# Five vector instructions at the opening of a feed-forward given to GpSimd

## What is computed

```python
    x = x + rmsnorm(ox @ p['x_wo'], nrm[3])
    h = rmsnorm(x, nrm[4])
    u, fconv_new = causal_dwconv(h @ p['f_wu'], fconv, p['f_conv_w'], p['f_conv_b'])
    x = x + rmsnorm((jax.nn.gelu(u) * (h @ p['f_wg'])) @ p['f_wd'], nrm[5])
```

## Time and profile before

| | us |
|---|---|
| median of three runs | 2245.98 (2242.68 to 2252.88) |
| the profiled execution, its own time | 2251.43 |
| its span, first to last instruction | 2249.4 |
| TensorE busy | 2160.9 (96%) |
| VectorE busy | 1285.9 (57%) |
| ScalarE busy | 841.4 (37%) |
| GpSimd busy | 619.2 (28%) |

### The profile page before, as it was taken

One profiled execution on the slowest core, in us unless ns is written; L12 is line 12 of the kernel. 1 busy time (PEld: TensorE's weight loads), 2 busy tenths in 40 slices (PEclk: granted clock), 3 DMA queues, 4 the chain that ended last, 5 costly groups with the idle time before them and its releaser, 6 DMA issues. The chain is left out here.

```text
span 2249.4 us, 42839 instructions
## 1 busy us (share of the span) xinstructions
PE 2160.9 (96%) x17101; PEld 1972.5 (88%) x17101; DVE 1285.9 (57%) x2350; ACT 841.4 (37%) x1720; POOL 619.2 (28%) x519
## 2 busy tenths in 40 slices
PE   9999998989999989999999999998899999999997
PEld 6799977866656689999999988998899999999997
DVE  5213354357776741232255254577898978866957
ACT  5222253126656730111343133554433334334453
POOL 5000035422323022111112200332344443345643
PEclk9999999879999999999999999998999999999998
DMA  4321097983545131110401354332232332264234
GB/s 145 107 61 44 29 204 243 311 284 124 167 135 171 71 120 43 61 57 29 162 29 38 121 198 188 99 114 86 91 124 91 105 110 72 106 238 170 93 125 146
DMA packets 133714, 276.35 MB, mean 123 GB/s; under 512 B 24626, under 2 KB 79571, under 8 KB 128332
## 3 DMA queue, kind: packets, MB, share of 16 engines
q1 hardware_dynamic: 110796, 232.32, 31.0%
q0 software_dynamic: 10368, 28.33, 3.9%
q10 hardware_dynamic: 12352, 12.96, 1.8%
HBM read 229.49 MB, written 48.26 MB: 123 GB/s over the span
## 5 line engine op out<-in xcount | busy, mean ns | idle before, releaser
L88 PE MATMUL psum<-merged_high,oq_half 128*128 128x352 f32 x768 | 189.0, 326 | 1.8 <-POOL oq_half L69 1.4
L88 PE MATMUL psum<-ff_t,ff_x_slots 128*128 128x264 f32 x1200 | 149.1, 284 | 1.3 <-DVE ff_x_slots L69 1.3
L88 PEld LDWEIGHTS psum<-ff_t,ff_x_slots 128*128 128x128 f32 x1200 | 147.1, 188 | 1.6 <-issue 1.5
L88 PEld LDWEIGHTS psum<-merged_high,oq_half 128*128 128x128 f32 x768 | 135.2, 190 | 2.5 <-POOL oq_half L69 1.9
L2006 ACT ACTIVATE na_pt<-psum 128x512 f32<-128x512 f32 (+1 forms) x170 | 86.8, 545 | 106.3 <-PE psum L1881 89.9
L88 PE MATMUL psum<-x_half_high,mg_w_high 128*128 128x352 f32 x384 | 124.0, 323 | 2.0 <-ACT gated L2390 1.2
L88 PE MATMUL psum<-h_again_low,mg_w_high 128*128 128x352 f32 x384 | 123.1, 321 | 0.0
L88 PE MATMUL psum<-x_half_high,mg_w_low 128*128 128x352 f32 x384 | 123.0, 320 | 0.0
L88 PE MATMUL psum<-ff_bslot,ff_x_slots 128*128 128x264 f32 x888 | 117.3, 285 | 0.7 <-DVE ff_z L4355 0.7
L69 POOL TENSOR_TENSOR ff_x_slots<-low,ff_x_slots 128x512 fp32r<-128x512 f32 x52 | 82.2, 1595 | 113.1 <-ACT ff_x_slots L3803 109.0
L88 PEld LDWEIGHTS psum<-ff_bslot,ff_x_slots 128*128 128x128 f32 x888 | 112.0, 189 | 1.0 <-DVE ff_z L4355 0.9
(11 more groups left out here) (668 smaller groups left out, 5604.7 us busy)
## 6 DMA issues: line engine op xcount, KB each, us to landing
na_kv<-in_pool POOLq DMA_DIRECT2D x128, 128.0 KB, 4.0
na_kv<-in_pool SPq DMA_DIRECT2D x128, 128.0 KB, 3.6
ff_bslot_raw<-mid_ops SPq DMA_DIRECT2D x59, 264.0 KB, 3.1
mid_ops<-ff_bufs SPq DMA_DIRECT2D x11, 1056.0 KB, 3.9
mg_w<-in_w_merge SPq DMA_DIRECT2D x15, 768.0 KB, 4.4
ring<-in_f_wu SPq DMA_DIRECT2D x11, 1024.0 KB, 5.4
low<-in_f_wg SPq DMA_DIRECT2D x22, 512.0 KB, 4.3
first_pages<-in_pool SPq DMA_DIRECT2D x68, 128.0 KB, 5.5
```

The costliest lines, as they stand in the source:

```text
L88: ins = nc.tensor.matmul(out, w[a], x[b], start=first and n == 0, stop=last and n == 2)
```

## The change

Five instructions of 128 x 1056 elements go from VectorE to GpSimd: the second half of t3's sum, both low parts of t3, and both low parts of t1. On GpSimd they stand behind the weight part 10 and ahead of the part 11. The tables follow. Nothing else is moved.

```diff
-        T_POOL, T_DVE = (("t3", 0),), (("t1", 0), ("t1", 1), ("t2", 0), ("t2", 1), ("t3", 1), ("t4", 0), ("t4", 1))
+        T_POOL, T_DVE = (("t3", 0), ("t3", 1)), (("t1", 0), ("t1", 1), ("t2", 0), ("t2", 1), ("t4", 0), ("t4", 1))
...
-        LOW_POOL = [("b22", 0)]
-        LOW_DVE = [("b11", 0), ("b21", 0), ("b11", 1), ("b21", 1), ("b22", 1), ("t2", 0), ("t2", 1), ("t3", 0), ("t3", 1), ("t1", 0), ("t1", 1),
-                   ("t4", 0), ("t4", 1)]
+        LOW_POOL = [("b22", 0), ("t3", 0), ("t3", 1), ("t1", 0), ("t1", 1)]
+        LOW_DVE = [("b11", 0), ("b21", 0), ("b11", 1), ("b21", 1), ("b22", 1), ("t2", 0), ("t2", 1), ("t4", 0), ("t4", 1)]
...
             low_of(10)
+            operand_low("t3", 0)
+            t_sum("t3", 1)
+            operand_low("t3", 1)
+            operand_low("t1", 0)
+            operand_low("t1", 1)
             for n in range(11, ND):
...
             operand_low("t2", 1)
-            t_sum("t3", 1)
             weight_low(0, 7)
-            operand_low("t3", 0)
             evac(2, "c11")
-            operand_low("t3", 1)
-            operand_low("t1", 0)
             evac(0, "u2")
-            operand_low("t1", 1)
             t_sum("t4", 0)
```

## The result

The change makes the kernel slightly slower. The median of the changed kernel is 2255.07 us (17 runs, 2246.74 to 2259.57) against 2246.97 us of the kernel before (17 runs, 2242.68 to 2253.95). The ratio on record is 1.0028, 95% interval [1.0019, 1.0038]: 6.3 us, with 4.3 and 8.5 as its ends. It is not the quotient of the medians, which lie 8.1 us apart (the means 7.2); the text goes by the ratio and its interval. The loss is within 0.5%, and the forecast was 4.9 us slower.

What follows compares the result with a forecast made beforehand. VectorE was taken to bound the opening; turn-taking waits of 10.75 us less 5.85 removed gave +4.9, carried whole to the end. On the median of 2245.98 that forecast 2250.9 us, range 2244 to 2255.5.

Steps and rivals of the forecast that it cites:

- relief in full: Rival: in the opening the engines overlap after all, so the change gains, -4.9 us, 2241.1; chance 0.09.
- mostly given back: Rival: turns fall better, or slack from 1579 to 1640 absorbs delay; +0 to +3 us, near 2247.5; chance 0.14.
- The price of a turn: In the opening, each GpSimd instruction of this shape takes 2.40 us, for which a waiting two-input VectorE instruction is blocked.
- The walk: Turn by turn through the opening: VectorE waits 10.75 us, less 5.85 removed, so block 1's weight sums come 4.9 late.
- The third turn: GpSimd's third, t3's second low part, 1561.1 to 1563.5: the weight part of (0,7) waits 2.4 us; (0,7) 4.9 late.
- rival 3: Behind a 5.8 us TensorE gap at 1554 the lower clock lasts over four products: +11.2 us, 2257.2 and more; chance 0.04.
- the wait of 1.15 at t4's first sum: GpSimd's fourth, 1564.1 to 1566.5: VectorE spends 1.3 us on two evacuations, then waits 1.15 with t4's first sum.
- the fifth: GpSimd's fifth instruction, 1567.7 to 1570.1: t4's second sum on VectorE waits 2.4 us.
- What was let go as free: Evacuations from PSUM run unslowed beside GpSimd at 0.70 us; load L3454, issued at about 1556, costs nothing.
- They take turns: Two-input SBUF instructions on VectorE and GpSimd never overlap: the later waits for the whole of the earlier, alternating when queues are full.
- the lower bound of +1.3: If two of five GpSimd turns meet only evacuations and one an idle queue, the opening ends +1.3 us.

Runs made afterwards that it cites:

- e1: Changed kernel with each of GpSimd's five moved instructions replaced by three fills that read nothing; 2243.77 us against 2249.07 for the kernel before, ratio 0.9974.
- e3: Kernel before with only t3's first low part and the second half of t3's sum moved to GpSimd; 2251.85 us in one run.
- e2: Kernel before plus five extra two-input subtractions on GpSimd, nothing moved; 2262.08 us, ratio 1.0045.
- e5: Kernel before with only t3's first low part moved to GpSimd; 2248.24 us.
- e7: Kernel before plus five extra GpSimd subtractions, the first waiting for t1's first sum; 2260.84 us in one run.
- e9: The changed kernel again, same code, for a second profile; 2252.75 us in one run.
- e8: Kernel before plus five extra two-input subtractions on GpSimd, nothing moved, the same program run once more; 2254.17 us in one run.

## Why the prediction was right, and where it was off

- **The bound and the place.** VectorE was the bound of the stretch, and its work moved one for one into the time: e1 got 4.78 back with the five gone and nobody reading; the rival "relief in full" would have been right if GpSimd's instructions were fills. The delay was carried on (4.53 at 1574, 4.88 at 1635, 3.98 and 5.48 at the end in two profiles, predicted 4.9), so "mostly given back" fell too.
- **The price of a turn.** Predicted 2.40 a turn from the earlier trace rows, measured 2.25 to 2.29 in all four rows. The estimate was 0.1 too high.
- **The walk.** Up to product (0,6) it holds: t2's low parts 11.12 us after t1's first sum (predicted 11.3), (0,6) at 12.51 (12.6). The third turn falls on the weight part, as predicted. Then it goes off in two places. (0,7) starts about 18.1 us after t1's sum, not 17.4, since it follows (0,6), which ran at the lower clock; I had put that gap into rival 3 and let it cost nothing in the forecast. And the wait of 1.15 at t4's first sum became 1.06 us of idle time on VectorE, spent waiting for TensorE, beside which GpSimd's fourth turn was free, while the fifth fell on t4's first sum, not on its second. The two sizes are so near that the sum hid it: (0,4) at 24.79 (predicted 25.0), the weight sums at 25.73 (26.15).
- **Rival 3, the clock.** Its start took place, its price did not. The lower level came behind the 5.56 us gap, as the Trainium skill has it in "TensorE: Matmul & The Clock Gate", Part 1 (idleness throttles, activity releases; the windows with 0.50, 0.68 and 1.00 agree), but it ended within (0,6) and (0,7), and VectorE was last from there on. It cost 1.0 us in e3. Here TensorE's lateness shows as 1.06 us of idle time on VectorE, but that stands where the walk has 1.15 of waiting for GpSimd's fourth: with (0,6) on time, t4's first sum would have been held to the end of GpSimd's fourth row at 1557.83, and it started at 1557.82. So the clock cost the stretch of the changed kernel next to nothing (an estimate from these rows), and not 6.3.
- **What was let go as free.** The evacuations stayed at 0.69 to 0.71 beside GpSimd. SyncE's load L3454 moved from 3.74 us after t1's first sum to 8.41, and no row waits for it:

```profile
1547.54 1.22 SPq L3453 DMA_DIRECT2D low<-in_f_wg  x2
```

- **"They take turns".** This step was right for this kernel and wrong as a rule. e2, e5, e7 and one place of e9 show VectorE passing GpSimd over. The forecast did not fail by it, since a turn not taken at once was taken at the next evacuation (e5, e9): GpSimd's work has to be let in somewhere before its result is due. Such a turn can be cheaper (e5 paid 1.6 for it, not 2.3); that I had only in the lower bound of +1.3.

By the runs, the interval of 4.3 to 8.5 us holds the 4.9 of the forecast, the 4.5 of the stretch and the 5.5 at the end of the second profile; the 4.0 of the first lies just below it. The mechanism and its size are borne out by the traces. That the median came to lie inside the stated range is partly luck: 2255.07 is 4.2 above the 2250.9 forecast and only 0.4 below the upper end of 2255.5, and no run explains that distance. The 3 us that the prediction allowed for the median of the runs was too little: the kernel before alone came out at 2245.98 by three runs and at 2246.97 to 2250.82 by 17 or 18.

## What to carry to other kernels

Before moving a two-input elementwise instruction from a full VectorE queue to an idle GpSimd, charge VectorE for GpSimd's whole duration, not for none: here each moved instruction saved 1.17 us and cost up to 2.3. By these rows it can pay only where GpSimd's reading falls beside PSUM evacuations or idle time of VectorE, or where the work given away only writes; of the runs, only the fills did pay.

## What the runs showed of the hardware that was not expected

- A GpSimd instruction that waits for its reads can be passed over for over 10 us by VectorE instructions that come back to back: its rows are 14.13 (e2), 12.79 (e7) and 12.93 us (e5), of which its own work is 2.4, so it waited for 10.4 to 11.7. It got in at the first evacuation from PSUM. The Trainium skill says in "SBUF — State Buffer", section "Who interferes with whom", that issue order decides who blocks. That does not cover these rows: in e7 the extra asked at 1548.58, and nine VectorE instructions that started from 1549.59 to 1557.80 went ahead of it.
- The same program did both (e2 and e8; the changed kernel's third instruction in its two profiles). In all twelve profiles GpSimd, where it was waiting, got the next turn behind a VectorE instruction that had itself been held. Behind one that had not, it got in at some places and not at others, and what decides there stays open.
- Fills on GpSimd held no VectorE row of e1's stretch, where GpSimd's first six fills (1547.07 to 1553.14) stood beside five full-size VectorE instructions.
- TensorE's clock went to its lower level behind a gap of 5.56 us, in the changed kernel and in e3. It cost e3 1.0 us and the changed kernel's stretch next to nothing, because VectorE and not TensorE was the bound a few us later.
